# When the convolution branch's sum of squares is closed: at the head of slot 14, or behind the attention step of the same slot

## The reference, cut to what matters

```python
def hybrid_mixer(h, w_in, ...):
    proj = h @ w_in
    pa, pq, pk, pv, pc, pg = jnp.split(proj, SPLITS, axis=-1)
    ya = conformer_branch(pa, ...)          # convolution branch
    yb = diff_attention_branch(pq, pk, pv, ...)
    yc = gmlp_branch(pc, ...)
    ...                                     # three gated products, summed, @ w_out

def conformer_branch(pa, conv_w, conv_b, ln_g, ln_b):
    glu = pa[..., :CONV_D] * jax.nn.sigmoid(pa[..., CONV_D:])
    c = causal_dwconv(glu, conv_w, conv_b)
    return jax.nn.silu(layer_norm(c, ln_g, ln_b))

def one_block(args):                        # of the attention branch, two maps m per head
    logits = jnp.einsum('bqhmd,bkhmd->bhmqk', q_blk, k) * scale + bias
    p = jax.nn.softmax(jnp.where(visible, logits, NEG_INF), axis=-1)
    attn = p[:, :, 0] - lam * p[:, :, 1]
    return jnp.einsum('bhqk,bkhe->bqhe', attn, v)
```

## Time and profile before

| | |
|---|---|
| time, median of 3 runs | 1855.88 us (1855.86 to 1862.45) |
| time of the profiled execution | 1855.88 us |
| its span, first to last instruction | 1854.1 us |
| mean granted TensorE clock | 0.992 |
| TensorE busy | 1799.5 us, 97% |
| VectorE busy | 1242.7 us, 67% |
| ScalarE busy | 727.0 us, 39% |
| GpSimd busy | 459.7 us, 25% |

### The profile page before, as it was taken

The page is one execution under the profiler, slowest core; times in us unless marked ns, Lnnn a source line. Parts: engine busy times, 40 slices in busy tenths (PEclk is TensorE's granted clock), DMA queues, the critical chain, the costliest instruction groups (busy, mean ns, idle before and its releaser), DMA issues. The chain is left out here.

```text
span 1854.1 us, 22430 instructions
## 1 busy us (share of the span) xinstructions
PE 1799.5 (97%) x8604; PEld 1494.0 (81%) x8604; DVE 1242.7 (67%) x1631; ACT 727.0 (39%) x942; POOL 459.7 (25%) x166
## 2 busy tenths in 40 slices
PE   9999999999979999999999999999998899999996
PEld 7888777888958788888789887788787687888885
DVE  6997656564548785586779666565644687685584
ACT  4232544433444443333423245443443544343341
POOL 3451100103004233443034400010020231434330
PEclk9999999999999999999999999999999999999998
DMA  6332122222311322222232322223232123222321
GB/s 250 118 135 92 69 103 80 110 107 91 136 46 69 124 88 108 91 95 97 104 136 92 124 81 75 97 78 135 91 113 84 59 98 117 91 92 94 111 91 46
DMA packets 28328, 186.10 MB, mean 100 GB/s; under 512 B 3480, under 2 KB 3608, under 8 KB 7740
## 3 DMA queue, kind: packets, MB, share of 16 engines
q1 hardware_dynamic: 26332, 172.64, 26.0%
q0 software_dynamic: 1648, 11.54, 1.7%
q10 hardware_dynamic: 240, 0.48, 0.1%
HBM read 179.33 MB, written 7.68 MB: 101 GB/s over the span
## 5 line engine op out<-in xcount | busy, mean ns | idle before, releaser
L1310 PE MATMUL ps<-x_hd,w_hd 128*128 128x512 f32 x1600 | 626.7, 392 | 6.4 <-DVE x_tl L794 2.7
L1311 PE MATMUL ps<-x_tl,w_hd 128*128 128x512 f32 x1600 | 623.1, 389 | 0.0
L475 POOL TENSOR_TENSOR w_tl<-raw,w_hd 128x2048 fp32r<-128x2048 f32 x78 | 361.1, 4629 | 510.6 <-ACT w_hd L598 418.8
L598 ACT ACTIVATE w_hd<-raw 128x2048 fp32r<-128x2048 f32 x155 | 297.3, 1918 | 286.5 <-PE ps L1311 233.3
L1320 PE MATMUL ps<-x_hd,w_tl 128*128 128x512 f32 x1600 | 381.6, 390 | 0.9 <-DVE w_tl L786 0.9
L1310 PEld LDWEIGHTS ps<-x_hd,w_hd 128*128 128x128 f32 x1600 | 300.4, 188 | 78.7 <-issue 4.8
L1320 PEld LDWEIGHTS ps<-x_hd,w_tl 128*128 128x128 f32 x1600 | 300.0, 188 | 63.5 <-DVE w_tl L786 1.4
L1311 PEld LDWEIGHTS ps<-x_tl,w_hd 128*128 128x128 f32 x1600 | 300.5, 188 | 61.6 <-issue 0.2
L786 DVE TENSOR_TENSOR w_tl<-raw,w_hd 128x2048 fp32r<-128x2048 f32 x78 | 179.1, 2296 | 122.6 <-ACT w_hd L598 75.3
L1310 PE MATMUL ps<-ring_hd,w_hd 128*128 128x512 f32 (+1 forms) x672 | 254.7, 383 | 3.8 <-DVE resid L1071 3.5
L1311 PE MATMUL ps<-ring_tl,w_hd 128*128 128x512 f32 (+1 forms) x672 | 252.3, 379 | 0.0
(11 more groups left out here) (160 smaller groups left out, 1557.6 us busy)
## 6 DMA issues: line engine op xcount, KB each, us to landing
raw<-units SPq DMA_DIRECT2D x155, 1024.0 KB, 4.8
resid<-x_t SPq DMA_DIRECT2D x4, 512.0 KB, 8.3
bias_t<-bias_tiles POOLq DMA_DIRECT2D x8, 256.0 KB, 4.5
cg<-mem_t POOLq DMA_DIRECT2D x2, 1024.0 KB, 5.1
resid<-x_t POOLq DMA_DIRECT2D x1, 2048.0 KB, 8.8
resid_dram<-resid POOLq DMA_DIRECT2D x1, 2048.0 KB, 9.7
resid<-resid_dram POOLq DMA_DIRECT2D x1, 2048.0 KB, 9.6
out<-resid SPq DMA_DIRECT2D x4, 512.0 KB, 2.8
```

The lines of the kernel that those rows point to most:

```text
L475: line.done(pool.tensor_tensor(w_tl[:, k % 2, :], raw[:, k % 2, :], w_hd[:, k % 2, :].bitcast(F32), ALU.subtract), of_unit("tail", g))
L598: line.done(act.activation(out, in_, func, **kw), *labels)
L1310: pe.matmul(dst, w_hd[:, slot, w], hd[:, src, :], start=kc == 0, stop=False)
L1311: i = pe.matmul(dst, w_hd[:, slot, w], tl[:, src, :], start=False, stop=False)
```

## The change

On DVE alone, and in both layers: the last addition of the sum of squares, `last_sum("c", KB)`, leaves the head of slot 14, and `mean_square("c", ms, 4, BR)` leaves its place ahead of `attention_last(k)`. Both now stand behind `attention_last(k)` of slot 14, that is behind `combine(0)`. No instruction is added or removed, and the lists of TensorE, ScalarE, GpSimd and the load queue are the same; what they wait for under the labels `c_all` and `c_ms` is now further back in DVE's list.

```diff
                 for k in range(NU):
-                    if k == CLN + 1:
-                        last_sum("c", KB)
                     if k == 36:
...
-                    if k == CLN + 1:
-                        mean_square("c", ms, 4, BR)
                     if k == CLN + 2:
                         for t in range(KB):
                             view = cg[:, C_OUT[t], PAD:]
                             op(lambda: dve.tensor_tensor(view, view, misc, ALU.mult), f"c_norm{t}", needs=("cb",))
                     attention_last(k)
+                    if k == CLN + 1:
+                        last_sum("c", KB)
+                        mean_square("c", ms, 4, BR)
```

## The result

The changed kernel takes 1884.48 us (median of 4, 1884.20 to 1885.04). The kernel before took 1859.16 beside it (median of 4, 1855.86 to 1863.56). The ratio is 1.0135, 95% interval 1.0107 to 1.0163: slower, as forecast, but 1.5 us above the upper end of the range of 1872 to 1883. The profiled execution of the changed kernel took 1885.28 us with a span of 1883.5, 29.4 more than the 1854.1 of before, at a mean granted clock of 0.980 instead of 0.992.

What follows compares the result with a forecast made beforehand. TensorE was taken to bound the kernel. On 1855.88 us: + 22.5 stall - 2.3 head 0's waits - 2.8 head 1's waits + 3.2 low clock = + 20.6, so 1876.5 us, range 1872 to 1883.

Steps and rivals of the forecast that it cites:

- What bounds the kernel, and the place of the stall: TensorE, busy 1799.5 of 1854.1 us, bounds; its column sums wait for the moved sum, 11.44 and 11.04 us, together 22.5.
- The part taken away: Head of slot 14: removing the sum gives nothing, since unit 16's tail still waits for ACT's head and starts at 194.55.
- What comes back: Shorter TensorE waits after the stall: 2.3 us before head 0's transposes, 2.8 before head 1's, over both layers.
- The chain: DVE and ACT work from the normalisation to head 1's transposes, said to carry a 1.4 us lead in each layer.
- the one on the clock: TensorE at half speed for 3.2 us behind each stall, 1.6 us lost, 3.2 for both; bounds nothing and 6.4.
- The base of the sum: Sum set against the profiled 1855.88 us; nothing counted after head 1's transposes, as TensorE's later waits move with its products.
- The signs of being wrong: Column sums before 207, clock low for longer than 6 us, or TensorE's waits between 260 and 1060 changing over a microsecond.
- The one that ends faster: Rival: DVE's 4.79 us idle for POOL at slot 14 is on the path and won; 1841.2 us, chance 0.02.
- the one that is paid back: Rival: TensorE finds 11 us less of waits in each layer; about 1856 to 1865 us, chance 0.03.
- Twice the low clock: Rival: double the clock loss behind the stalls, 1879.7 us; chance 0.17 shared with no lead for head 1.
- a gate stuck at a quarter: Rival: low clock sticks, reckoned at 0.50 from each stall to head 1's transposes; up to 1957 us, chance 0.02.
- its worst sum: Rival case of no lead for head 1 and twice the low clock together, 1882.5 us; within the shared chance 0.17.

## Why the forecast missed

**What bounds the kernel, and the place of the stall: right.** TensorE has no slack, and what its column sums were late went into the time. Forecast were waits of 11.44 and 11.04 us, measured starts that are 11.5 and 11.1 later.

**The part taken away: right.** The tail of unit 16 starts at 194.66 behind 6.20 us of idle, against 194.55; it still waited for ACT's head, and nothing was won.

**What comes back: right, in both parts.** Head 0's transposes gave 1.5 and 1.1 (1.31 and 0.96 forecast), head 1's 1.5 in each layer (1.4 forecast), and the remaining wait in layer 1 is 0.72 (0.7 forecast). The chain is the one forecast too: counted from unit 16's start at 220.82, the normalisation begins 0.84 us after it (about 0.5 forecast) and ACT's next step 2.17 (2.15). The run with unit 17's tail moved got the second part on its own.

**The step that failed** is the one on the clock, in two terms. The first: "I take 3.2 us at half speed behind each stall, a little more than the row, since the column sums are light work: 1.6 us lost, 3.2 for both." Measured are 7.4 and 6.5 us at the low level, and 3.5 + 3.2 = 6.7 us lost, the "double, 6.4" that I had as the bound. One row of one execution doesn't give the length of a low clock: in the runs here it is 3.2 to 8.3 us behind a long stall. The reason given didn't hold either: light work behind the stall was not shown to lengthen it. This term was 3.5 us too small, and that alone would have put the sum at 1880.0, inside the range.

**The base of the sum** was the second and larger term, and it had been put at nothing. "After head 1's transposes I count nothing" is right for waits, and the waits there are indeed the same. It leaves out that the clock falls in the gaps of both kernels, and not equally in each execution: 5.6 us in the profiled pair. The 29.4 us of that pair are the 20.6 of the sum, 3.5 and 5.6, less 0.3 of small differences. The profiled execution of before belonged to the better of two groups, which has 21 of 64; the shown runs of before were 1855.88, 1862.45 and 1855.86, and the 1862.45 was a sign of it that I passed over. Against the usual 1862 the change costs 22.5 us, against the better group 28. That 22.5 is near the 20.6 is partly luck, since with the right low clock at the stalls the sum would have been 24.1.

**The signs of being wrong.** Of the three that were named, the column sums didn't start before 207 and the waits between 260 and 1060 us didn't change by a microsecond. The clock did stay low for longer than 6 us, behind both stalls: that sign came, and it points at the term that was too small.

**The rivals.** The one that ends faster and the one that is paid back did not show. "Twice the low clock" at 1879.7 was the case that came, together with the base. The Trainium skill's warning of a gate stuck at a quarter ("TensorE: Matmul & The Clock Gate", section "Seeing it yourself"; the rival itself reckoned with 0.50) did not show either: with the clock back 8.3 us behind the stalls at the latest, no profiled execution here has anything like it. The same page, in the section "What's actually happening", says of the return to the full clock at a kernel's start that it varies from run to run, and that its cost is below 1% of a typical span and not worth fitting. The falls here are not at the start, but their size agrees: 1861.4 less 1848.9 is 0.7% for the kernel before. But a change of 1% is then of the same size, and the difference can't be left out.

**Chances.** Slower had 0.94. The range should have gone to 1887 or so: 1882.5 for its worst sum, and the 5 to 6 us by which executions of the unchanged kernel differ.

## What to carry to other kernels

When an instruction is moved back in an engine's list, look for the label that it carries, not for the engine's own busy time: 0.69 us of DVE work that moved by 13 us stopped another engine for 11, since the label was only 1.8 us ahead of need. A stall of TensorE of some microseconds costs more than its length, by the slower work behind it: 3.2 to 3.5 us behind the stalls of 11 us in the pair compared here, and 3.4, half of 6.8, behind one of 3.3 us. Work that nobody reads in a gap that can't be closed gets most of this back, and here it made the kernel before 12.5 us faster and its executions alike. And before a sum is set on one profiled execution, its clock and its place among the runs should be looked at: two groups of times in three runs are a warning that the base itself can be off by more than the terms.

## What had not been expected of the hardware

- The clock falls at gaps that are far shorter than the 4 us rows that I had read: after a wait of 1.73 us in the feed-forward block the stretch from 637 to 641 has 0.75 in one execution and 1.00 in another of the same kernel.
- It can fall after TensorE is back at work, and not in the gap: 0.4 us after the restart at 638.61 in that execution, and 2.0 us after the restart at 207.37 behind the fillers.
- The unchanged kernel has two groups of times, 1855.9 to 1858.0 and 1861.2 to 1863.7, that go with the mean granted clock; with its gaps filled it has one, 1848.1 to 1849.9.
- Filling a gap with float32 matmuls of 128x512 (22 recorded instructions in 9.61 us for 11 matmuls) holds the clock at the full level while they run, and mostly behind them: of the four stalls filled with 11 of them, in two traces, two still had a fall behind the 1.4 to 1.8 us left idle. These fillers moved the start of the work behind them by about 0.2 us at most where it is shown above.
- Behind stalls of 11 us the low clock lasted between 3.2 and 8.3 us, and 6.8 us behind a wait of 3.3. What sets this is open. Putting the heavy matmuls ahead of the light ones gave 5.5 and 4.0 us in the medians, but no shorter low clock behind the first stall.
